# The delta rule's gate projections, dealt in parts over the steps of attention

## The reference

```
proj = h @ w_in                      # h: normed and modulated x
q_a, k_a, v_a, q_d, k_d, v_d, z_d, b_d, a_d = split(proj)
y_attn  = dilated_attention(q_a, k_a, v_a, rel_bias)        # 8 heads of 64
qkv     = silu(causal_conv([q_d, k_d, v_d]))                # 8 heads of 64
o       = chunk_gated_delta_rule(l2norm(q), l2norm(k), v, g, beta)
y_delta = rmsnorm(o) * silu(z_d)                            # z_d: the gate
x = x + g1 * (concat([y_attn, y_delta]) @ w_out)
```

## Time and profile before

| | |
|---|---|
| median of three runs | 2802.22 us |
| profiled execution | span 2803.8 us (the page gives the span alone) |
| TensorE matmul busy | 2729.2 us, 97% |
| VectorE / ScalarE busy | 1441.8 us, 51% / 1135.0 us, 40% |
| mean granted TensorE clock | 0.991 |
| jobs and attention, 192 to 262 us | two gate jobs to 214.5, attention to 262 |

### The profile page before, as it was taken

One profiled execution on the slowest core, in us unless ns is written; L12 is line 12 of the kernel. 1 busy time (PEld: TensorE's weight loads), 2 busy tenths in 40 slices (PEclk: granted clock), 3 DMA queues, 4 the chain that ended last, 5 costly groups with the idle time before them and its releaser, 6 DMA issues.

```text
span 2803.8 us, 39113 instructions
## 1 busy us (share of the span) xinstructions
PE 2729.2 (97%) x16710; PEld 2176.3 (78%) x16710; DVE 1441.8 (51%) x1870; ACT 1135.0 (40%) x1395; POOL 222.5 (8%) x205
## 2 busy tenths in 40 slices
PE   6999989999999999999999999999999999999998
PEld 4876867888877777677788888887786777888886
DVE  6586657443466664445574444555543455633322
ACT  4375344222244533546442222355425454422221
POOL 0012310000022100001010001010100010100001
PEclk8999999999999999999999999999999999999999
DMA  6531014433332133222243433321241212222221
GB/s 259 196 135 55 4 62 161 162 139 128 124 130 81 61 134 133 87 106 83 98 156 144 149 133 143 117 91 68 89 164 50 90 68 73 87 104 105 87 98 57
DMA packets 46308, 309.00 MB, mean 110 GB/s; under 512 B 5551, under 2 KB 6063, under 8 KB 12600
## 3 DMA queue, kind: packets, MB, share of 16 engines
q1 hardware_dynamic: 44152, 296.62, 28.7%
q0 software_dynamic: 1984, 9.89, 1.1%
HBM read 302.27 MB, written 2.12 MB: 109 GB/s over the span
## 4 chain that ended last, share of the span: by engine, by line
PE 91%; DVE 3%; ACT 2%; issue 1%; DMA 1%; POOL 1%; SPq 0%; DVEq 0%; ACTq 0%; POOLq 0%
PE bank L2333 69%; PE bank L2266 5%; PE bank L2467 2%; PE bank L2707 2%; PE bank L2678 2%; PE bank L2316 2%; PE bank L2834 1%; DMA raw<-in_wstream_dram 1%; DVE WL L1588 1%; PE bank L2693 1%; PE bank L2723 1%; PE bank L2395 1%; ACT WH L985 1%; DVE raw L1626 0%; POOL eadd L860 0%
## 5 line engine op out<-in xcount | busy, mean ns | idle before, releaser
L2333 PE MATMUL bank<-HH,WH 128*128 128x512 f32 x2208 | 889.2, 403 | 10.0 <-DVE HL L1706 5.5
L2333 PE MATMUL bank<-HH,WL 128*128 128x512 f32 x2208 | 861.8, 390 | 0.0
L2333 PE MATMUL bank<-HL,WH 128*128 128x512 f32 x2208 | 861.5, 390 | 0.0
L1588 DVE TENSOR_TENSOR WL<-raw,WH 128x2048 fp32r<-128x2048 f32 (+2 forms) x263 | 484.9, 1850 | 560.6 <-ACT WH L985 560.4
L985 ACT ACTIVATE WH<-raw 128x2048 fp32r<-128x2048 f32 (+2 forms) x220 | 395.0, 1795 | 338.9 <-PE bank L2333 303.3
L2333 PEld LDWEIGHTS bank<-HH,WH 128*128 128x128 f32 x2208 | 415.4, 188 | 118.4 <-issue 22.5
L2333 PEld LDWEIGHTS bank<-HL,WH 128*128 128x128 f32 x2208 | 415.6, 188 | 90.1 <-issue 8.4
L2333 PEld LDWEIGHTS bank<-HH,WL 128*128 128x128 f32 x2208 | 415.2, 188 | 88.0
L2333 PE MATMUL bank<-AH,WH 128*128 128x512 f32 x492 | 191.4, 389 | 0.0
L2333 PE MATMUL bank<-AL,WH 128*128 128x512 f32 x492 | 191.4, 389 | 0.0
L2333 PE MATMUL bank<-AH,WL 128*128 128x512 f32 x492 | 191.4, 389 | 0.0
(11 more groups left out here) (408 smaller groups left out, 3462.0 us busy)
## 6 DMA issues: line engine op xcount, KB each, us to landing
raw<-in_wstream_dram SPq DMA_DIRECT2D x256, 1024.0 KB, 4.8
raw<-in_wstream_dram SPq DMA_DIRECT2D x24, 512.0 KB, 3.3
raw<-in_wstream_dram SPq DMA_DIRECT2D x12, 768.0 KB, 4.3
bgam<-in_consts_dram POOLq DMA_DIRECT2D x2, 1792.0 KB, 7.2
xT<-in_x_dram SPq DMA_DIRECT2D x2, 1024.0 KB, 7.9
bturn<-bqk POOLq DMA_DIRECT2D x8, 256.0 KB, 4.3
out_dram<-ost SPq DMA_DIRECT2D x4, 512.0 KB, 2.7
toep<-bias_dram POOLq DMA_DIRECT2D x6, 256.0 KB, 4.0
```

The lines of the kernel that those rows point to most:

```text
L1588: TT(WL[:, wi % 2, now], raw[:, j.load % RAW, now], WH[:, wi % 2, now].bitcast(F32), ALU.subtract).then_inc(s["w_split"], 2 if half is Non ...
L2333: last = MM(o[m][:, :], a, b, start=j.first and u == 0 and q == 0, stop=j.last and u == j.units - 1 and q == 2)
```

## The change

The two `zd` jobs leave their place between conv and attention. Each is cut in 16 parts of three products (one unit of one bank), and `GATE_STEPS` tells in which attention step TensorE issues each of the 32: four in steps 0 and 1, then 2, 3, 2, 1 by turns up to step 13, between the transposes and AV. They accumulate in bank 3, one half job at a time; ScalarE copies each finished half to `zs` (steps 2, 6, 10, 14). AV has bank 2 alone, so it waits for VectorE's subtraction of the pair before. Since the parts still read `HH` and `HL`, the first two finished pairs go to places of their own, and GpSimd's queue moves them by DMA once the parts are through. ScalarE and VectorE split the weights of the job behind each gate job at steps 3 and 14, and 5 and 17. Silu is done on all of `zs` at once in the delta rule (p = 1, l = 3). The two ada chunks of the gate jobs go to the jobs i = 3 and 4 of the projection; `length`, `unit` and the last conv Silu close up behind the conv jobs. Some semaphores are joined.

```diff
+GATE_STEPS = [0] * 4 + [1] * 4 + [g + x for g in (2, 6, 10) for x in (0, 0, 1, 1, 1, 2, 2, 3)]
...
+        if kind == "zd":
+            continue
         job(kind, 0, i, every=2 if kind == "conv" else 1)
+        if i in (3, 4):
+            ada_chunk()
...
-                  11: [("length", 3), ("unit", 2)], 12: [("conv", 6), ("unit", 3)]}.get(i, [])
+                  11: [("length", 3), ("unit", 2), ("conv", 6), ("unit", 3)]}.get(i, [])
     for t in range(20):
         steps.append(("attn", t))
+        for z in range(2):
+            if t == GATE_STEPS[16 * z]:
+                steps.append(("job", "zd", 0, 12 + z))
...
+            return (early_high[:, pair, :], early_low[:, pair, :]) if pair < 2 else (HH[:, pair, :], HL[:, pair, :])
...
+                if st == ("attn", 12):
+                    pool.wait_ge(s["a_low"], 2)
+                    pool.wait_ge(s["gemm_done"], JOBS[GATES[1]].w + 1)
+                    pool.dma_start(HH[:, 0:2, :], early_high[:, :, :]).then_inc(s["a_moved"], 16)
+                    pool.dma_start(HL[:, 0:2, :], early_low[:, :, :]).then_inc(s["a_moved"], 16)
...
-                elif kind == "zd":
-                    for m in range(2):
-                        put(zs[:, 2 * (i - 12) + m, :], o[m][:, :], ACT.Silu)
...
+                for z in range(2):
+                    for m in range(2):
+                        if t == GATE_STEPS[16 * z + 8 * m + 7] + 1:
+                            if m == 0:
+                                act.wait_ge(s["gemm_half"], z + 1)
+                            else:
+                                act.wait_ge(s["gemm_done"], JOBS[GATES[z]].w + 1)
+                            A(zs[:, 2 * z + m, :], bank[3][:, :], ACT.Copy).then_inc(s["zd_out"], 1)
...
-                    A(HH[:, pair, :], bank[2 + pair % 2][:, :], ACT.Copy).then_inc(s["a_high"], 1)
+                    A(attended(pair)[0], bank[2][:, :], ACT.Copy).then_inc(s["a_high"], 1)
...
+                act.wait_ge(s["a_moved"], 32)
                 token_copy(0)
...
                         A(dX[:, :], bank[1][:, :], ACT.Copy).then_inc(s["d_xc"], 1)
+                        if p == 1 and l == 3:
+                            act.wait_ge(s["zd_out"], 4)
+                            A(zs[:, :, :], zs[:, :, :], ACT.Silu).then_inc(s["zd_out"], 1)
+                            ready_ln(ACT.Exp)
...
                 elif st[0] == "attn":
+                    for z in range(2):
+                        if st[1] == (3, 14)[z]:
+                            begin(GATES[z])
...
+                for z in range(2):
+                    if t == (5, 17)[z]:
+                        begin(GATES[z])
...
+                if t >= 7 and t % 4 == 3:
+                    pair = (t - 7) // 4
+                    high, low = attended(pair)
+                    dve.wait_ge(s["a_high"], pair + 1)
+                    TT(low, bank[2][:, :], high.bitcast(F32), ALU.subtract).then_inc(s["a_low"], 1)
...
+            def gate_part(x):
+                z, m, u = x // 16, x // 8 % 2, x % 8
+                j = JOBS[GATES[z]]
+                if m == 0 and u == 0:
+                    pe.wait_ge(s["w_split"], 2 * (j.w + 1))
+                if u == 0:
+                    if x:
+                        pe.wait_ge(s["zd_out"], 2 * z + m)
+                    else:
+                        pe.wait_ge(s["act_evac"], JOBS[LAST_IN].act)
+                wh, wl = (w[:, j.w % 2, u * CW + P * m:u * CW + P * m + P] for w in (WH, WL))
+                for k, (a, b) in enumerate(((wh, HH[:, u, :]), (wh, HL[:, u, :]), (wl, HH[:, u, :]))):
+                    last = MM(bank[3][:, :], a, b, start=u == 0 and k == 0, stop=u == 7 and k == 2)
+                if u == 7:
+                    last.then_inc(s["gemm_done" if m else "gemm_half"], 1)
...
+                for x in range(32):
+                    if GATE_STEPS[x] == t:
+                        gate_part(x)
...
-                    if i == 0 and p >= 2:
-                        pe.wait_ge(s["a_low"], p - 1)
+                    if i == 0 and p:
+                        pe.wait_ge(s["a_low"], p)
...
-                            last = MM(bank[2 + p % 2][64 * e:64 * e + 64, P * i:P * i + P],
+                            last = MM(bank[2][64 * e:64 * e + 64, P * i:P * i + P],
```

More of the change, by code:

```diff
@@ L274, in jobs_of @@
         j.act0, j.dve0 = act, dve
-        if j.last:
+        if kind == "zd":
+            j.bank = -1
+        elif j.last:
             bank += 1
@@ L300 @@
 STEPS, FILLED = plan()
-EMBEDDED = {n for x in FILLED.values() for n, _ in x}
+EMBEDDED = {n for x in FILLED.values() for n, _ in x} | {n for n, x in enumerate(STEPS) if x[:2] == ("job", "zd")}
 LOADS, JOBS, PRODUCTS, FREED, WTOTAL = jobs_of(STEPS)
@@ L445, in spare @@
             return nc.alloc_sbuf_tensor_at(name, [P, S], F32, offset=16512 + 2048 * (KD * t + k))
-        toeps = [toep[:, x, :] for x in range(3)] + [spare("toep_late", 1, 4)[:, :]]
+        toeps = [toep[:, x, :] for x in range(3)] + [arena("toep_late", 14, [S])[:, :]]
+        early_high, early_low = arena("early_high", 40.25, [2, S], F32R), arena("early_low", 48.25, [2, S], F32R)
         dQK = [spare("dQK0", 1, 6), arena("dQK1", 58.25, [S]), arena("dQK2", 56.25, [S]), CO[:, 0, :]]
@@ L731, in program, with attended @@
         ATTENTION = STEPS.index(("attn", 0))
+        GATES = [STEPS.index(("job", "zd", 0, 12 + z)) for z in range(2)]
+        def attended(pair):
+            return (early_high[:, pair, :], early_low[:, pair, :]) if pair < 2 else (HH[:, pair, :], HL[:, pair, :])
         TOKENS = [(0, 0), (1, 2), (1, 0), (0, 1), (1, 1), (0, 2), (1, 3), (0, 3)]
@@ L970, in _, with ready_ln @@
             ready = [0]
-            def ready_ln():
+            def ready_ln(f=ACT.Ln):
                 if ready[0]:
                     act.wait_ge(s["table"], ready[0])
-                A(table_col[:, :], eps[:, :], ACT.Ln).then_inc(s["table"], 1)
+                A(table_col[:, :], eps[:, :], f).then_inc(s["table"], 1)
                 ready[0] += 1
@@ L998, in bias @@
             def bias():
-                act.wait_ge(s["bias_ps"], 1)
+                act.wait_ge(s["n_bias_ps"], 1)
                 A(bias_row[0:8, 0:512], bank[6][0:8, :], ACT.Copy).then_inc(s["bias_rows"], 1)
@@ L1018, in shift_high @@
                 if r:
-                    act.wait_ge(s["n_bias_ps"], r)
+                    act.wait_ge(s["n_bias_ps"], r + 1)
                 else:
@@ L1240, in attention @@
                     act.wait_ge(s["a_out"], 4 * pair + 4)
-                    if pair == 0:
-                        act.wait_ge(s["gemm_done"], gemm_before(ATTENTION))
-                    A(HH[:, pair, :], bank[2 + pair % 2][:, :], ACT.Copy).then_inc(s["a_high"], 1)
+                    if pair == 2:
+                        act.wait_ge(s["gemm_done"], JOBS[GATES[1]].w + 1)
+                    A(attended(pair)[0], bank[2][:, :], ACT.Copy).then_inc(s["a_high"], 1)
             def token_copy(i):
@@ L1453, in final_root @@
                 act.wait_ge(s["e_sum"], 1)
-                A(er[:, :], bank[6][:, :], ACT.Ln, bias=eps[:, :], scale=1.0 / D).then_inc(s["e_ln"], 1)
-                act.wait_ge(s["e_ln"], 1)
-                A(er[:, :], er[:, :], ACT.Exp, scale=-0.5).then_inc(s["e_rstd"], 1)
+                A(er[:, :], bank[6][:, :], ACT.Ln, bias=eps[:, :], scale=1.0 / D).then_inc(s["e_root"], 1)
+                act.wait_ge(s["e_root"], 1)
+                A(er[:, :], er[:, :], ACT.Exp, scale=-0.5).then_inc(s["e_root"], 1)
             GB, ADDS = [0], [0]
@@ L1730, in evacuate @@
                     if j.w in HALVED and m == 0:
-                        dve.wait_ge(s["gemm_half"], HALVED.index(j.w) + 1)
+                        dve.wait_ge(s["gemm_half"], 2 + HALVED.index(j.w) + 1)
                     else:
@@ L1831, in attention @@
                            ).then_inc(s["a_norm"], 1)
[L1832 to L1836, removed]
             def delta(begin_):
@@ L1925, in gated @@
                     dve.wait_ge(s["df_cp"], q + 1)
+                    dve.wait_ge(s["zd_out"], 5)
                     if q:
@@ L2161, in _ @@
                     if st[1] == 3:
-                        dve.wait_ge(s["e_rstd"], 1)
+                        dve.wait_ge(s["e_root"], 2)
                     for k in range(4 * (st[1] - 3), 4 * (st[1] - 3) + 4):
@@ L2552, in out_product @@
                         pe.wait_ge(s["a_low"], 4)
+                        pe.wait_ge(s["a_moved"], 32)
                         pe.wait_ge(s["d_ud"], 16)
@@ L2599, in delta @@
                             pe.wait_ge(s["a_low"], 4)
+                            pe.wait_ge(s["zd_out"], 4)
                         if l > 1:
@@ L2735, in bias @@
                 MM(bank[7][0:8, 0:P], relb[0:33, :], onehot[0:33, 512:TOEP], start=True, stop=True
-                   ).then_inc(s["bias_ps"], 1)
+                   ).then_inc(s["n_bias_ps"], 1)
             nrm = 0
```

15 lines of the change are left out of this document (6 added, 9 removed).

## The result

The changed kernel takes 2809.43 us (median of 7 runs, 2807.21 to 2815.99) where the kernel before takes 2801.68 beside it: a ratio of 1.0027, 95% interval 1.0017 to 1.0037. A second measurement gave 1.0031 (1.0019 to 1.0043). So it is slower, by 7.7 us; 2809 was predicted. The profiled execution spans 2805.9 us.

What follows compares the result with a forecast made beforehand. TensorE, holding 91% of the chain, was taken to bound the kernel, attention included. Start -10.6, twelve steps +13.5, end +3.1 and Silu +1.1 sum to +7.1 us: median 2809, range 2800 to 2815.

Steps and rivals of the forecast that it cites:

- The start: From the last conv job to attention's first transposes: gate jobs leave, half clock follows a gap; -10.6 us, bounds -13.3 and -9.
- T0: Mark of attention's first transposes on TensorE, at 218.70 us before; expected near 208.
- The twelve steps: Attention from the first transposes to the last pair's: added parts and waits less absorbed time; +13.5 us, bounds +10.5 and +17.
- I take -2.5, nearest to that row: In the twelve attention steps, long products hide fixed gaps of small TensorE groups: -2.5 us, from 0 to -5.4.
- the waits: Steps 2, 6 and 10: parts beginning bank 3 anew wait for ScalarE's copy, 1.2 us three times, +3.6.
- the slack: Half clock and waits within the twelve attention steps before, absorbed by a TensorE never out of work: -3.9 us.
- The end: Attention from step 14 on: ScalarE sets the pace and AV has one bank; +3.1 us, bounds +1 and +4.
- the bank: End of attention: AV of the last pair, with one bank for two, waits over 2 us for VectorE's subtraction.
- Silu: Delta rule, ScalarE between two dX copies: 4.7 us of work in 3.62 free; +1.1 us, bounds +0.5 and +2.
- Gaps close: Rival: TensorE's small groups lose all fixed waits, -5.4 us, and the clock stays up; total +1.5, 2804 us; chance 0.34.
- Room after all: Rival: softmax paces attention's steps, so the 24 parts cost nothing; -9.1 us, 2793; chance 0.08.
- Loses step: Rival: VectorE's normalizing in steps 7 and 11 and split in step 5 uncovered; +13 us, 2815; chance 0.10.

Runs made afterwards that it cites:

- copy-first: Changed kernel with ScalarE copying the finished half out of bank 3 ahead of the step's PT copies: 2808.81 us, 1.0019 of the kernel before.
- one-product: Changed kernel with two of three products left out in each of the 24 parts of steps 2 to 13: 2800.32 us.
- before with the row sums early: Kernel before with GpSimd's growth of the second pair moved ahead of the third mask, behind the last transposes: 2796.26 us.
- the kernel of all edits: Changed kernel with every edit that gained something, plus GpSimd's growth of the second pair behind the last transposes: 2797.26 us.

## Why the prediction came out right, step by step

**The start** was forecast at -10.6 and measured -10.7, with the hole (4.59 us until ScalarE's Ln), the half clock and T0 at 208.0 as written. The forecast put 2.7 us on twelve products at half clock; these took 1.9 more (4.63 for 2.72) and the scores ahead of them 0.6 (1.66 for 1.05).

**The twelve steps** were put at +13.5 and took +15.4. This step held the wrong choice: "I take -2.5, nearest to that row", for small groups whose fixed 0.15 us a long product would hide. They stayed: two, four, six and eight transposes take 0.39, 0.58, 0.81 and 1.04 in the chain. The other terms held: 24 parts at 0.69 are 16.6, the waits 1.08, 1.11 and 1.02 are 3.2, the slack absorbed 3.9; together 15.9 for 15.4. The copy-first and one-product runs show waits and products each at their price.

**The end** was +3.1 and measured +2.6: from the last pair's transposes to the row sums 18.9 for 16.4. ScalarE's queue was named rightly (the split, the zs copy, Exp, the copy), the bank was not: AV waited 1.68 for the subtraction, not over 2, and alone the bank was worth 0.25 to 0.5. And one cause was missed. I cost the two moves at nothing by what their transfers would delay; but they wait for the last part in GpSimd's queue, so the growth of the first pair behind them went from 233.85 in the trace before to 253.08, onto VectorE's normalizing. What stands behind a waiting instruction I had worked out for TensorE alone. In the trace before, the same growth had lengthened another `tensor_scalar` of VectorE, ahead of the normalizing for which TensorE then waits:

```profile
234.57 1.40 DVE L1823 TENSOR_SCALAR anmax<-amax 128x2 f32<-128x2 f32 x1
```

```profile
237.01 1.09 PE L2429 MATMUL bank<-ident,Sx 128*128 128x128 f32 x8 [1.13 <-DVE Sx L1830]
```

That instruction takes 0.17 elsewhere. So by these rows 1.13 of the 3.9 us that the prediction called half clock and waits came from the growth, and the move carried the collision from the twelve steps to the end. VectorE's half of the split fell into its idle time as written, against the earlier trace rows the wait for the copy is 0.75, formerly 2.95:

```profile
266.88 2.28 DVE L1621 TENSOR_TENSOR WL<-raw,WH 128x2048 fp32r<-128x2048 f32 x1
269.91 0.69 DVE L1864 TENSOR_TENSOR HL<-bank,HH 128x512 fp32r<-128x512 f32 x1 [0.75 <-ACT HH L1268]
```

**Silu** was +1.1 and measured +1.06. The load ends at 310.71 and Silu begins at 310.73, so here too no drain stands behind it, against the Trainium skill (ScalarE: Activation LUTs, section What ACT_TABLE_LOAD costs).

**The sum** up to the Silu, without the clock behind the row sums, is thus 7.3 + 1.06, 8.3, for 7.1 forecast; the medians' 7.7, with an interval of 4.8 to 10.4 us, fits both. The spans of single profiles can't carry the comparison: before had half clock at the row sums and at 374 to 381, some 2.9 us each, which no profile of the changed kernel shows at the second place, while that kernel had it at the end and at the row sums, 2.9 each, in one profile and not in the other. By one pair of profiles the spans differ by 2.1, by the other (2814.4 and 2803.3) by 11.1. Runs of like mean clock are the better pairs: in the changed kernel's second measurement and before beside it they differ by 7.4 at 0.994 (2807.8 and 2800.4), 6.2 at 0.993, 4.2 at 0.992 and 8.9 at 0.991, each from few runs. So the loss is the change's own and no difference of clock. I had used the row of half clock only for the start and not asked whether the other falls would stay.

**The rivals.** Gaps close: a pair took 14.4 to 15.4, not under 12.7. Room after all: the one-product run refutes it. Loses step: no step 5, 7 or 11 shows TensorE waiting for VectorE. That forecast and median agree to 0.4 us is partly luck: the twelve steps were undersized by 1.9 and the end oversized by 0.5, and single runs of the changed kernel spread over 2807.2 to 2816.0.

**What stays open**: why the clock falls behind the same hole of 2.94 us in one execution and not in another, and why before with the row sums early, and the kernel of all edits, kept full clock also where their edits change nothing. One or two profiles of each kernel can't tell chance from cause there. The mean clocks say only that it was more than one execution: all 22 runs of these two kernels have 0.993 or more, where 10 of the 21 of before beside them have 0.991 or 0.992.

## What to carry to other kernels

Ask of each stage which engine paces it before dealing work into it: where TensorE's pieces stand end to end in the chain, a product costs its full time wherever it is put, and only holes take work for free (16 parts at the start came as early as eight). When a step is moved past a queue, follow the queue of the idle engines too: GpSimd, 8% busy, cost VectorE 1.9 us where the moves had pushed its work and 1.2 where it stood before, and moving one line of its queue, with a wait of its own, closed the hole of 2.94 us, in the fastest kernel of all. And compare profiles from a common mark, with the granted clock beside it, and runs at like mean clock, before a difference of spans is explained.

## What the runs showed of the hardware

Unexpected was how much of such a difference is clock: the same program, the same hole of 2.94 us, and row sums at 1.12 in one execution and 2.07 in the next, with 2.9 us lost behind. Two 128x256 `tensor_scalar` on VectorE took 2.54 us beside two GpSimd products, 0.61 without; one of 128x2 took 1.40 and 1.02 beside them, 0.17 without. The bias instructions of VectorE beside the same products kept their time (0.28 of 128x128, 0.69 of 128x512).
